# A one-core decoder-layer kernel: weight-block sums of the up-projection as additions, two of four formed by accumulating DMAs issued from GpSimd

## The reference

```python
def conv_glu_ffn(h, w_up, conv_w, conv_b, w_down):
    u = h @ w_up
    c = lax.conv_general_dilated(u, conv_w[:, None, :].astype(u.dtype), window_strides=(1,),
                                 padding=[(CONV_WIDTH - 1, 0)],
                                 dimension_numbers=('NWC', 'WIO', 'NWC'),
                                 feature_group_count=2 * D_FF) + conv_b
    gate, val = jnp.split(c, 2, axis=-1)
    return (jax.nn.gelu(gate, approximate=True) * val) @ w_down
```

## Time and profile before

| | |
|---|---|
| time, median of 3 runs | 2064.43 us (2063.61 to 2065.13) |
| profiled execution, its own time | 2064.49 us |
| its span in the trace | 2062.7 us |
| TensorE busy | 1998.8 us, 97% |
| VectorE busy | 1545.6 us, 75% |
| ScalarE busy | 1012.3 us, 49% |
| GpSimd busy | 0.7 us |
| bytes moved by DMA | 323.26 MB |

### The profile page before, as it was taken

The page is one execution under the profiler, slowest core; times in us unless marked ns, Lnnn a source line. Parts: engine busy times, 40 slices in busy tenths (PEclk is TensorE's granted clock), DMA queues, the critical chain, the costliest instruction groups (busy, mean ns, idle before and its releaser), DMA issues.

```text
span 2062.7 us, 31761 instructions
## 1 busy us (share of the span) xinstructions
PE 1998.8 (97%) x12510; PEld 1796.4 (87%) x12510; DVE 1545.6 (75%) x2028; ACT 1012.3 (49%) x1549; POOL 0.7 (0%) x6
## 2 busy tenths in 40 slices
PE   8999999999999889999999999999999999999994
PEld 6888888888887789999999999999999787878773
DVE  5522543445446889898898889888998998899998
ACT  7422433435435655555555555545555554554442
POOL 0000000000000000000000000000000000000000
PEclk9999999999999999999999999999999999999998
DMA  8433232211636534324423432442344776668793
GB/s 317 138 123 118 77 93 82 82 62 62 244 124 211 177 103 160 119 100 151 149 101 121 163 117 100 136 163 101 111 145 154 237 245 211 224 214 295 254 361 125
DMA packets 218895, 323.26 MB, mean 157 GB/s; under 512 B 9134, under 2 KB 140622, under 8 KB 216444
## 3 DMA queue, kind: packets, MB, share of 16 engines
q1 hardware_dynamic: 218076, 315.99, 45.0%
q10 hardware_dynamic: 672, 5.24, 0.6%
HBM read 292.60 MB, written 32.54 MB: 158 GB/s over the span
## 4 chain that ended last, share of the span: by engine, by line
PE 83%; DVE 10%; issue 3%; ACT 3%; DMA 1%; DVEq 0%; SPq 0%; ACTq 0%
PE ring L2034 11%; PE ring L2036 11%; PE ring L2035 11%; PE ring L2295 9%; PE ring L2297 9%; PE ring L2296 9%; PE side L2295 4%; PE side L2297 4%; PE side L2296 4%; PE side L2034 2%; PE side L2035 2%; PE side L2036 2%; DVE w_lo L1721 2%; DVE raw L1730 1%; PE side L2110 1%
## 5 line engine op out<-in xcount | busy, mean ns | idle before, releaser
L1442 DVE TENSOR_TENSOR w_lo<-raw,w_hi 128x512 fp32r<-128x512 f32 x256 | 169.7, 688 | 275.2 <-ACT w_hi L1027 275.2
L1721 DVE TENSOR_TENSOR w_lo<-q,w_hi 128x1024 fp32r<-128x1024 f32 (+1 forms) x262 | 308.3, 1177 | 79.7 <-ACT w_hi L1244 69.5
L2295 PE MATMUL ring<-s_hi,w_hi 128*128 128x256 f32 x1008 | 286.8, 284 | 6.7 <-ACT snaps L1336 3.5
L2296 PE MATMUL ring<-s_lo,w_hi 128*128 128x256 f32 x1008 | 286.4, 284 | 0.0
L2297 PE MATMUL ring<-s_hi,w_lo 128*128 128x256 f32 x1008 | 286.4, 284 | 0.0
L1721 DVE TENSOR_TENSOR w_lo<-raw,w_hi 128x1024 fp32r<-128x1024 f32 x214 | 249.3, 1173 | 37.1 <-ACT w_hi L1244 26.9
L1027 ACT ACTIVATE w_hi<-raw 128x512 fp32r<-128x512 f32 x256 | 151.8, 624 | 187.7 <-PE ring L2036 171.1
L1244 ACT ACTIVATE w_hi<-q 128x1024 fp32r<-128x1024 f32 x174 | 183.6, 1056 | 97.5 <-PE side L2297 54.2
L2295 PEld LDWEIGHTS ring<-s_hi,w_hi 128*128 128x128 f32 x1008 | 194.8, 193 | 7.3 <-ACT snaps L1336 3.9
L2295 PE MATMUL ring<-a_hi,w_hi 128*128 128x256 f32 x688 | 195.3, 284 | 4.0 <-issue 3.3
L2034 PE MATMUL ring<-w_hi,act_hi 128*128 128x512 f32 x488 | 192.9, 395 | 3.3 <-DVE w_lo L1442 2.7
(11 more groups left out here) (298 smaller groups left out, 4672.8 us busy)
## 6 DMA issues: line engine op xcount, KB each, us to landing
q<-in_w_up SPq DMA_DIRECT2D x65, 1024.0 KB, 5.0
q<-in_w_down SPq DMA_DIRECT2D x66, 512.0 KB, 4.5
raw<-in_w_down SPq DMA_DIRECT2D x66, 512.0 KB, 4.5
raw<-in_w_in SPq DMA_DIRECT2D x28, 1024.0 KB, 5.4
raw<-in_w_out SPq DMA_DIRECT2D x24, 1024.0 KB, 4.9
raw<-in_w_up SPq DMA_DIRECT2D x23, 1024.0 KB, 6.9
q<-sa_d SPq DMA_DIRECT2D x22, 512.0 KB, 4.4
raw<-in_w_mem_kv SPq DMA_DIRECT2D x8, 1024.0 KB, 7.1
```

What stands on the lines that cost most here:

```text
L1442: dve.tensor_tensor(w_lo[:, s, q], raw[:, s, q], w_hi[:, s, q].bitcast(F32), ALU.subtract).then_inc(lo_done, 1)
L1721: dve.tensor_tensor(lo, src, hi.bitcast(F32), ALU.subtract).then_inc(hp_lo_done, 1)
L2295: pe.matmul(dst, hi, b_hi, start=first, stop=False, skip_group_check=True)
L2296: pe.matmul(dst, hi, b_lo, start=False, stop=False, skip_group_check=True)
```

## The change

All four T become additions: T1 = B11 + B12, T2 = B22 + T1, T3 = B12 + B22, T4 = B21 + T2. It is the same form with half of the blocks taken with the other sign, and the minus signs move elsewhere. The weights of P1 are negated while they are split (ScalarE's copy gets a scale of -1, and VectorE's low part is computed as minus the source, minus the high part). S2 changes its sign, S1 is a difference in place of a sum, and the joining of the parts changes signs to match.

From chunk 2 on T1 and T3 are no longer formed by VectorE. GpSimd issues for each a DMA that adds one SBUF tile into another (`accum_op=ALU.add`): T1 = B11 + B12 into the tile of B11, when the low parts of both halves of P1 are done (they read B11), and T3 = B12 + B22 into the tile of B12, when T1 has landed (its DMA reads B12). Their semaphores are `t1_in` and `t3_in`. `t_ready` gives the semaphore and value that readers of a T wait for. VectorE forms T2 in slot 0 of its own chunk, ahead of the low part of slot 4, which is made from T2, and T4 in slot 5 as before.

```diff
+        def t_ready(c, name):
+
+            if c > 1 and name in ("T1", "T3"):
+                return (t1_in, t3_in)[name == "T3"], 16 * (c - 1)
+            return t_done, t_count(c, name)
...
@@ gpsimd
+            for c in range(2, CHUNKS):
+                pool.wait_ge(hp_lo_done, place(c, P1, 1) + 1)
+                pool.wait_ge(*b_landed("12", c))
+                pool.dma_start(b11_at(c)[:, :, :].rearrange("p k n -> p (k n)"),
+                               b12_at[:, :, :].rearrange("p k n -> p (k n)"), accum_op=ALU.add).then_inc(t1_in, 16)
+                pool.wait_ge(*b_landed("22", c))
+                pool.wait_ge(t1_in, 16 * (c - 1))
+                pool.dma_start(b12_at[:, :, :].rearrange("p k n -> p (k n)"),
+                               raw[:, 0, :], accum_op=ALU.add).then_inc(t3_in, 16)
...
@@ hp_to_hi
-                    act.wait_ge(t_done, t_count(c, {FROM_T2: "T2", FROM_T1: "T1", FROM_T3: "T3",
-                                                    FROM_T4: "T4"}[p]))
+                act.wait_ge(*t_ready(c, {FROM_T2: "T2", FROM_T1: "T1", FROM_T3: "T3", FROM_T4: "T4"}[p]))
                 act.activation(hp_hi[:, h % 4, :].rearrange("p (k n) -> p k n", n=P), hp_source(h),
-                               ACT.Copy).then_inc(hp_hi_done, 1)
+                               ACT.Copy, scale=-1.0 if p == P1 else 1.0).then_inc(hp_hi_done, 1)
...
@@ make_t
-            def minus(dst, a, b):
-                dve.tensor_tensor(dst, a, b, ALU.subtract).then_inc(t_done, 1)
+            def total(dst, a, b):
+                dve.tensor_tensor(dst, a, b, ALU.add).then_inc(t_done, 1)
...
                 elif name == "T2":
                     dve.wait_ge(hp_lo_done, place(c - 1, P4, 1) + 1 if c else 2)
                     dve.wait_ge(*b_landed("22", c))
-                    dve.wait_ge(t_done, t_count(c, "T1"))
-                    minus(t2, b22, t1)
+                    dve.wait_ge(*t_ready(c, "T1"))
+                    total(t2, b22, t1)
...
@@ hp_to_lo
-                dve.tensor_tensor(lo, src, hi.bitcast(F32), ALU.subtract).then_inc(hp_lo_done, 1)
+                if h < H_DOWN and SEQ[h][1] == P1:
+                    dve.scalar_tensor_tensor(out=lo, in0=src, scalar=-1.0, in1=hi.bitcast(F32), op0=ALU.mult,
+                                             op1=ALU.subtract).then_inc(hp_lo_done, 1)
+                else:
+                    dve.tensor_tensor(lo, src, hi.bitcast(F32), ALU.subtract).then_inc(hp_lo_done, 1)
...
@@ VectorE's after(w)
                 if w == 14:
                     make_t(1, "T2")
+                if 1 < c < CHUNKS and s == 0:
+                    make_t(c, "T2")
...
-                    if 1 < c < CHUNKS - 1 and s in (11, 12, 13):
-                        make_t(c + 1, ("T1", "T2", "T3")[s - 11])
-                    if c == 1 and s in (12, 13):
-                        make_t(c + 1, ("T1", "T2")[s - 12])
-                    if c == 2 and s == 0:
-                        make_t(c, "T3")
```

More of the change, by code:

```diff
@@ L558, in build @@
         hp_hi_done, hp_lo_done, hp_used = sem("hp_hi_done"), sem("hp_lo_done"), sem("hp_used")
-        t_done = sem("t_done")
+        t_done, t1_in, t3_in = sem("t_done"), sem("t1_in"), sem("t3_in")
         c11_kept = sem("c11_kept")
@@ L649, in t_count @@
         def t_count(c, name):
-            order = ("T1", "T3", "T2", "T4") if c == 0 else ("T1", "T2", "T3", "T4")
-            return 4 * c + order.index(name) + 1
+            if c < 2:
+                order = ("T1", "T3", "T2", "T4") if c == 0 else ("T1", "T2", "T3", "T4")
+                return 4 * c + order.index(name) + 1
+            return 2 * c + 4 + ("T2", "T4").index(name) + 1
+        def t_ready(c, name):
+            if c > 1 and name in ("T1", "T3"):
+                return (t1_in, t3_in)[name == "T3"], 16 * (c - 1)
+            return t_done, t_count(c, name)
         def hp_source(h):
@@ L913, in load_item @@
                 elif where < 4:
-                    sp.wait_ge(t_done, 4 * CHUNKS)
+                    sp.wait_ge(*t_ready(CHUNKS - 1, "T4"))
                     sp.wait_ge(hp_lo_done, place(CHUNKS - 1, P5, 1) + 1)
@@ L941, in _ @@
                 else:
-                    sp.wait_ge(t_done, 4 * c)
+                    sp.wait_ge(*t_ready(c - 1, "T4"))
                     load_down(0)
@@ L946, in _ @@
                 if 0 < c < CHUNKS - 2:
-                    sp.wait_ge(t_done, 4 * c + 4)
+                    sp.wait_ge(*t_ready(c, "T4"))
                     load_b("11", c + 2, b11_at(c + 2))
@@ L1456, in make_t @@
                     dve.wait_ge(*b_landed("12", c))
-                    minus(t1, b12, b11_at(c)[:, :, :])
+                    total(t1, b12, b11_at(c)[:, :, :])
                 elif name == "T2":
@@ L1469, in make_t @@
                         dve.wait_ge(*b_landed("22", c))
-                    minus(b12, b22, b12)
+                    total(b12, b22, b12)
                 else:
@@ L1473, in make_t @@
                     dve.wait_ge(hp_lo_done, place(c, P6, 1) + 1)
-                    minus(t2, b21_at(c)[:, :, :], t2)
+                    total(t2, b21_at(c)[:, :, :], t2)
             def turn_to_lo(n, dst, hi, gain):
@@ L1766, in sum_s1 @@
                 add(batch_of(by_token_tile(s1_val[:, :, :]), batch), batch_of(a21, batch), batch_of(a22, batch),
-                    ALU.add)
+                    ALU.subtract)
             def sum_s2(batch):
@@ L1771, in sum_s2 @@
                 dve.wait_ge(x1_out[2], 16)
-                add(batch_of(by_token_tile(s2_val[:, :, :]), batch), batch_of(by_token_tile(s1_val[:, :, :]), batch),
-                    batch_of(a11, batch), ALU.subtract)
+                add(batch_of(by_token_tile(s2_val[:, :, :]), batch), batch_of(a11, batch),
+                    batch_of(by_token_tile(s1_val[:, :, :]), batch), ALU.subtract)
             def sum_s3():
@@ L1828, in c11 @@
                     dst = u_gate[:, f, 0:HALF_S]
-                dve.tensor_tensor(dst, y_bank(f), snaps[:, 0, f, :], ALU.add).then_inc(c11_done, 1)
+                dve.tensor_tensor(dst, y_bank(f), snaps[:, 0, f, :], ALU.subtract).then_inc(c11_done, 1)
             def c22(c, f):
@@ L1834, in c22 @@
                     dve.wait_ge(tapped, 4 * (c - 1) + 3 + f)
-                dve.tensor_tensor(u_val[:, f, HALF_S:S], v_bank(f), snaps[:, 2, f, :],
-                                  ALU.add).then_inc(c22_done, 1)
+                dve.tensor_tensor(u_val[:, f, HALF_S:S], snaps[:, 2, f, :], v_bank(f),
+                                  ALU.subtract).then_inc(c22_done, 1)
             def c21(c, f):
                 dve.tensor_tensor(u_gate[:, f, HALF_S:S], v_bank(f), snaps[:, 1, f, :],
-                                  ALU.add).then_inc(c21_done, 1)
+                                  ALU.subtract).then_inc(c21_done, 1)
             def taps(c, val, f):
```

## The result

The changed kernel takes 2068.74 us (median of 20 runs, 2066.43 to 2070.3), the kernel before 2065.58 us (20 runs in the same comparison, 2063.33 to 2067.18). The ratio is 1.0016, 95% interval 1.0009 to 1.0023: about 3.2 us slower, clear of zero and under the 0.2% that the prediction called a change. The prediction said 2064.5, range 2061 to 2112.

A forecast was written before the change was run, and what follows sets the result against it. TensorE bounds the kernel, busy all 95.00 us of an up-projection window. VectorE's relief, signs, T2's move and the DMAs each counted 0 on the profiled 2064.49 us: forecast 2064.5, range 2061 to 2112, its own range 2062.5 to 2067.

The forecast's parts named there:

- VectorE's relief: Up-projection, chunks 2 to 21: taking 40 additions (91 us) off VectorE gains 0 to 0.5 us, taken as 0.
- the signs: P1's negated copy and low parts, other sign edits: nothing on the path; chunks 0 and 1 cost 0 to 0.8 us.
- L: Time from when T1's DMA may be issued until T1 has landed: taken as 7.6 us, bounds 4.9 and 13.1.
- the limit: Longest time T1's DMA may take before TensorE stalls, in each of 20 chunks: 9.7 us, from 6.0 plus 3.7.
- the low part alone: Path from T2 through slot 4's low part to TensorE: cover left 3.7 us after T2's earliest start.
- chunk 2: First chunk with the DMAs: T2's turn at about 799.2, so L may be 8.9 before VectorE stands; nothing new.
- rival 1: Adding DMA takes over 9.7 us, so TensorE waits 20 times: 2076 to 2156 us; chance 0.41 together with Rival 2.
- Rival 2: GpSimd's DMA preparation is held up by VectorE: L 10.1, 8 us in all, 2072; chance 0.41 together with rival 1.
- Rival 3: A lighter VectorE shortens the rest: needs over 4.1 us, only 1 or 2 by a lucky shift; chance 0.04.

## Why the prediction was right, and where it was not

- **Right: VectorE's relief is worth nothing.** 40 sums went, 13 us in 95, and TensorE's windows stay full. The kernel with T3 alone by DMA shows it once more at 0.9999.
- **Right: the signs.** "At most 0.8 us"; measured -0.8 with an interval of 1.9 us on either side.
- **Right in kind, a little high: L.** The prediction had 7.6 us, made of 2.1 fixed and two passes of 2.75. In chunk 10 P1's low part ends at 1116.1 and T2 starts at 1123.4, so L is 7.3. The parts are 4.6 for a copy from issue to landing, 2.3 for the addition, and some 0.3 before the issue begins. What the prediction worked out for two reads from the Trainium skill's page "DMA: Bandwidth & Descriptors" (its anatomy of one DMA on the gpsimd path), an estimate of 6.8 us, is close to the 6.9 measured. What the Trainium skill's "Collectives: The Full Stack" says of inline additions (why ReduceScatter is half of AllGather) is in line with it: adding costs 2.3 us on a copy's 4.6, though no run here tells the second read from the adding itself.
- **Wrong: the limit.** The step reads "TensorE stalls only if L is over 6.0 + 3.7 = 9.7 us". Measured, the offset may be 2.3 us, so L about 8.3. The sentence that failed is the one before it, that what stands behind T2 has "one to three slots of room more than T2 itself". That was priced along the low part of slot 4 and not along the chain taps, GELU, snapshot of slot 4. The chain crosses from VectorE to ScalarE and from there to TensorE, and it ends 1.2 us sooner than the path through the low part. For the low part alone 3.5 were measured against 3.7.
- **Wrong: chunk 2.** "T2's turn comes at about 799.2, and L may be 8.9 there". I took ScalarE's copy for one that had waited for slot 0. In the trace of before that slot ended at 795.07, and the copy had waited for T2:

```profile
795.07 0.39 ACT L1336 ACTIVATE snaps<-ring 128x256 f32<-128x256 f32 x1 [0.69 <-PE ring L2297]
799.23 1.06 ACT L1244 ACTIVATE w_hi<-raw 128x1024 fp32r<-128x1024 f32 x1 [3.77 <-DVE raw L1446]
```

  The room there was 795.1 - 790.3 = 4.8 us, less than in the other chunks (6.0), and this is the chunk that loses most. (A slip without effect: in the earlier trace rows T2, at 1116.16, is VectorE's second sum of three, not the third.)
- **Missed: the spread of L.** One value was used for 20 transfers. Sixteen were on time. Four landed 1 to 2 us later than the rest, and the waits are with them: the trace puts about 1.6 us of lost time in chunk 2 (the distance of two issues of T1, 41.90 us against 40.32), 0.5 in chunk 5 and 0.4 in chunk 11. The prediction read the one packet of 0.02 MB in the earlier trace rows as an empty DMA queue; it is one of the instruction queue (`q8 instruction: 1, 0.02, 0.5%`), the kind found beside every late transfer.
- **Outcome.** The forecast with its own range, 2062.5 to 2067, missed the 2068.7; of the 4.2 us between them 3.2 are the change and 1.1 the kernel before, which took 2065.58 in the comparison and not 2064.49. The wide range held it by luck of its width. It was wide for rival 1, and rival 1 in its own terms did not happen: no L was over 9.7 (the longest was 9.3, in chunk 2), and the slot that waited most was not slot 4. Its mechanism, a VectorE that stands at T2 until TensorE waits, did, in a few chunks and over a path that no rival named. Rival 2 (GpSimd held up by VectorE) finds no support: with VectorE about as busy a copy lands in 4.6 us, less than SyncE's loads (5.0). Rival 3 did not happen.

No version that computes the layer beats the kernel before by more than the interval. With the GELUs one half product later the change costs nothing, and brings nothing.

## What to carry to other kernels

Before moving work to a DMA, ask whether the engine that it relieves is waited for; here TensorE had one wait of 0.5 us in 800, so only latency could change the time. When a wait enters an engine's queue, follow what stands behind it across every engine until it reaches the one that sets the end: the tightest path need not be the one for which the waiting instruction works, and reordering one instruction on a third engine (here a GELU behind a snapshot) can be worth all of the loss. Allow for the slowest transfer, and prove a margin by making the transfer late on purpose: one such run gave the limit to about 0.1 us.

## What the runs showed of the hardware

- An adding DMA of 1 MB from SBUF to SBUF, 128 rows of 8 KB, lands 6.9 us after issue (median of 40; 6.8 to 9.0), a copy by the same queue in 4.6, a load of `w_up` into the same kind of tile by SyncE's queue in 5.0 (65 of them; the 23 into `raw` take 6.5).
- The add moves in eight bursts with idle gaps, the copy without (one transfer of each looked at).
- All 40 adding transfers that took more than 7.8 us, of 257 in seven kernels, had a 0.02 MB packet of the instruction queue in flight; none of the 164 without one took longer. The cause was not tried.
- After waits of TensorE of 4.0, 2.4 and 2.0 us the granted clock was 0.51, 0.64 and 0.68 over the next 4 to 7 us; after one of 2.9 us (the kernel before) and one of 2.5 us (T1 one slot late, chunk 12) it was 1.00.
- GpSimd is busy 0.86 us for each adding DMA and 0.53 for each copy.
- A SCALAR_TENSOR_TENSOR over 1024 columns takes 1225 ns, the plain subtraction 1222.
